# Where the slot-table products stand among the shared expert's projections in a two-layer hybrid trunk step

## Chip, cores and metric

## What is computed

The reference runs two layers over 128 context tokens and 512 latent tokens of width 1024. Each layer has a mixer sub-layer (differential attention, a bidirectional state-space branch and neighbourhood attention) and a channel sub-layer. The change touches only the channel sub-layer:

```python
def moe_ffn(h, p):
    t = h.reshape(-1, d)
    s = jax.nn.sigmoid((t @ p["w_router"]).astype(jnp.float32))
    _, idx = lax.top_k(s + p["b_router"].astype(jnp.float32), TOP_K)
    sel = jnp.take_along_axis(s, idx, axis=-1)
    w = sel / jnp.sum(sel, axis=-1, keepdims=True) * ROUTE_SCALE
    ...
    routed = jnp.einsum("nef,efd->nd", jax.nn.silu(hg) * hu * gates[:, :, None], p["w_e_down"])
    shared = (jax.nn.silu(t @ p["w_s_gate"]) * (t @ p["w_s_up"])) @ p["w_s_down"]
    return (routed + shared).reshape(bn, l, d)
```

There are 32 routed experts with hidden width 128, of which every token takes four, and one shared expert with hidden width 256.

## The kernel before

Each engine has its own instruction stream, written out by hand in program order; the streams meet only at semaphores. Each layer passes a chain of stages. The change is in `stage_tail` (from line 2321), which does the output projection, the norm, the router, the shared expert's two input projections and then all routed experts. `stage_combine` follows it.

**Routing.** VectorE turns router scores into a choice mask, ranks and counts (lines 2840 to 2966). Experts are sorted by token count into 8 groups of 4, one expert for each 32-row lane. Each chosen (token, expert) pair gets a slot. Two one-hot arrays encode it: `where` (the slot tile, L2937 on VectorE and then L2475 on GpSimd, semaphore `where_ready`) and `place` (the position within 128 slots, L2943 on VectorE, semaphore `place_ready`; it lies in the buffer `late`). TensorE multiplies them: 20 products of 128x128 weights by 60 columns summed into PSUM bank 6 (L2611), then `table_mm`. VectorE turns that sum into token numbers and destinations (L2957 to L2966, `table_known`).

**Shared expert.** `shared_lat(c, up)` (L2569, matmuls on L2572) is one projection of the 512 latent tokens: 8 matmuls, one for each k, with 128x128 weights of ring slot 3 and 512 columns, into a PSUM bank of its own (bank 4c + up). Four such calls exist: (0,0), (0,1), (1,0), (1,1). After (0,1) and after (1,1) TensorE raises `shared_mm`; ScalarE answers with Silu (L2741, L2742), and VectorE with the product (L2835, L2836, `shared_hid`).

**TensorE's order around the change** (L2600 to L2617): (0,0), (0,1), two small transposes (L2604), (1,0), then waits for `place_ready` and `where_ready`, the table products, (1,1), `shared_mm`, and `slots_free` raised to 2. Then come `turn(0)` and `turn(1)` (L2619, transposes on L2627), each behind the gather of its 128 rows (`xg_ready0`, `xg_ready1`), and the loop over the expert groups: `up` (L2640), `turn_hidden` (L2647), `turn` of a later tile, `down` (L2658).

**GpSimd** waits for `table_known` and issues two indirect gathers from `h_rows` (L2483), then `gather(2)` and `gather(3)` (L2451), each of which waits until the tile two before it has been transposed. Each gather brings up to 128 rows of 4 KB into `xg` (in the buffer `mixT`). They use DMA queue q0.

**SyncE** loads expert weights over queue q1 (`load_up` L2414, `load_down` L2419; 512 KB each, 12 for each group): group 0 once the experts are known, group 1 once `slots_free` is 2 (it overwrites the shared weights), and each later group once the group two before has passed TensorE. **ScalarE** loads gate rows over queue q10 (L409 to L411) after `turned(1)` and `table_known`.

Of the kernel before, what the change touches and what calls it, by code (L numbers as in the profile page):

```python
# [22 lines left out]
KT = D // P  # L23
# [2297 lines left out]
def stage_tail(nc, cx, L, m, x):  # L2321
# [3 lines left out]
    sem = cx.sem  # L2325
    ps = cx.ps
    with ExitStack() as st:
# [170 lines left out]
        def _(pe):  # L2498
# [67 lines left out]
            pe.sem_inc(sem("slots_free"), 1)  # L2566
            sh = section_ready(cx, pe, ("shared_up", 0)).rearrange("p (k n) -> p k n", k=KT)

            def shared_lat(c, up):  # L2569
                a = up * SFF + c * P  # L2570
                for k in range(KT):
                    ins = pe.matmul(ps[:, 4 * c + up, :], sh[:, k, a:a + P], cx.hT[:, k, CTX:TOK], start=(k == 0),  # L2572
                                    stop=(k == KT - 1))
                return ins

            def shared_ctx(c):
# [21 lines left out]
                sem("rank_mm"), 1)  # L2598
            rows_high(TILES - 1)
            shared_lat(0, 0)  # L2600
            shared_lat(0, 1).then_inc(sem("shared_mm"), 1)
            pe.wait_ge(sem("ids_ready"), 1)
            for j in range(2):
                ins = pe.transpose(ps[0:1, 7, j * P:(j + 1) * P], ids[:, j:j + 1], cx.ident)  # L2604
            ins.then_inc(sem("ids_turned"), 1)
            shared_lat(1, 0)
            pe.wait_ge(sem("rows_high_out"), TILES)
            pe.wait_ge(sem("place_ready"), 1)
            pe.wait_ge(sem("where_ready"), 1)
# [1 line left out]
                ins = pe.matmul(ps[:, 6, 0:TABLE], place[:, n, :], where[:, n, :], start=(n == 0),  # L2611
                                stop=(n == N_CHOICE - 1))
            ins.then_inc(sem("table_mm"), 1)
            shared_lat(1, 1).then_inc(sem("shared_mm"), 1)
            pe.wait_ge(sem("shared_mm"), 2)
            pe.sem_inc(cx.ring_free, 1)
            pe.sem_inc(sem("slots_free"), 1)  # L2617
# [774 lines left out]
```

## Time and profile before

| | before |
|---|---|
| runs | 2551.98, 2555.4, 2559.52 us |
| median | 2555.4 us |
| profiled execution, its own time | 2552.58 us |
| its span in the trace | 2550.8 us |
| TensorE matmul busy | 2374.8 us, 93% |
| VectorE, ScalarE, GpSimd busy | 938.5, 647.4, 412.6 us |
| mean granted TensorE clock | 0.972 of full |

The trace covers the span; the profiled execution's own time is 1.8 us more. Times in timelines count from the start of the span. The channel sub-layer's table products start at 1041.86 us in the first layer and at 2258.22 us in the second. A granted clock of 1.00 is 2.4 GHz, 0.50 is 1.2 GHz.

### The profile page before, as it was taken

How to read it: one execution, taken by the hardware profiler on the slowest of the kernel's cores; microseconds unless marked ns; L12 is line 12 of the kernel's file. 1: busy time of each engine (PE TensorE's matmuls, PEld its weight loads, DVE VectorE, ACT ScalarE, POOL GpSimd, SP SyncE). 2: the span in 40 equal slices, each digit the busy share in tenths (PEclk: the TensorE clock that was granted, in tenths of full speed). 3: DMA queues.
4: the chain of work that ended last, by engine and by line, in shares of the span. 5: the costliest groups of instructions: out<-in, count | busy, mean ns of one | idle time of the engine just before them, and what ended most of it. 6: DMA issues, size and time to landing. Idle time of an engine off the chain costs nothing. (4 is left out here: it accounts for less than half of the span.)

```text
span 2550.8 us, 36359 instructions
## 1 busy us (share of the span) xinstructions
PE 2374.8 (93%) x13824; PEld 1413.1 (55%) x13824; DVE 938.5 (37%) x1813; ACT 647.4 (25%) x1574; POOL 412.6 (16%) x488
## 2 busy tenths in 40 slices
PE   7999999999998999899879999999999899989995
PEld 4446644566457655555455565556655765555552
DVE  2513412552007334422365153246300743452226
ACT  2224401450015013022132252037001501302221
POOL 0003100030003300133410030002100230013333
PEclk8999999999999999899989999999999999989997
DMA  9443145100644220689652220220042322065985
GB/s 348 173 164 102 58 169 214 42 1 33 213 137 110 72 70 34 262 328 401 250 216 88 87 104 33 85 74 1 33 131 76 107 86 70 34 234 207 374 333 221
DMA packets 170190, 368.37 MB, mean 144 GB/s; under 512 B 38836, under 2 KB 52156, under 8 KB 170052
## 3 DMA queue, kind: packets, MB, share of 16 engines
q1 hardware_dynamic: 121604, 261.23, 27.9%
q10 hardware_dynamic: 24768, 54.82, 6.1%
q0 software_dynamic: 23680, 50.43, 5.9%
q8 instruction: 91, 1.49, 0.2%
q14 instruction: 47, 0.39, 0.0%
HBM read 343.99 MB, written 47.56 MB: 154 GB/s over the span
## 5 line engine op out<-in xcount | busy, mean ns | idle before, releaser
L224 PE MATMUL ps<-hT,ring 128*128 128x512 f32 x496 | 222.9, 603 | 5.6 <-PEq L1242 2.7
L233 PE MATMUL ps<-ring,hT 128*128 128x512 f32 x480 | 213.5, 602 | 5.6 <-PEq L1286 4.4
L2640 PE MATMUL ps<-ring,mixT 128*32 128x256 f32 x2688 | 212.5, 379 | 0.6 <-DMA ring<-in_w_e_up 0.4
L2640 PEld LDWEIGHTS ps<-ring,mixT 128*32 128x32 f32 x2688 | 119.4, 110 | 92.9 <-issue 18.1
L224 PEld LDWEIGHTS ps<-hT,ring 128*128 128x128 f32 x496 | 92.8, 192 | 124.0 <-issue 123.9
L233 PEld LDWEIGHTS ps<-ring,hT 128*128 128x128 f32 x480 | 90.8, 192 | 117.8 <-issue 115.9
L1389 PE MATMUL ps<-late,ring 128*128 128x320 f32 x512 | 144.1, 440 | 3.7 <-PEq L1907 2.5
L2508 PE MATMUL ps<-ring,mixT 128*128 128x512 f32 x320 | 140.4, 598 | 4.4 <-PEq L1286 4.4
L1389 PEld LDWEIGHTS ps<-late,ring 128*128 128x128 f32 x512 | 98.1, 193 | 47.6 <-issue 8.2
L756 PE MATMUL ps<-hT,ring 128*128 128x512 f32 x256 | 114.5, 601 | 2.9 <-ACT ssm_dec L1011 2.9
L2658 PE MATMUL ps<-ring,ex_hidT 128*32 128x512 f32 x768 | 115.4, 598 | 0.8 <-DMA ring<-in_w_e_down 0.8
L2010 PE MATMUL ps<-hT,ring 128*128 128x512 f32 x256 | 113.3, 595 | 0.3 <-issue 0.3
L1352 PE MATMUL ps<-mix_T,mix_S 128*128 128x320 f32 x384 | 107.2, 434 | 1.8 <-POOL mix_S L1340 1.2
L2508 PEld LDWEIGHTS ps<-ring,mixT 128*128 128x128 f32 x320 | 60.8, 192 | 79.1 <-issue 79.1
L1949 POOL DMA_DIRECT2D na_raw<-rpb_scratch x64 | 38.1, 598 | 398.9 <-DVE na_bias L2250 291.0
L1352 PEld LDWEIGHTS ps<-mix_T,mix_S 128*128 128x128 f32 x384 | 72.5, 190 | 34.3 <-POOL mix_S L1340 2.2
L1580 POOL TENSOR_SCALAR da_co<-da_sm,da_rc,da_ls 128x1 f32<-128x1 f32 x32 | 11.0, 344 | 480.3 <-DVE da_rc L1864 480.3
L2978 DVE TENSOR_TENSOR ex_hid<-ps,ex_silu 128x128 f32<-128x128 f32 x60 | 17.5, 292 | 188.3 <-ACT ex_silu L2755 188.3
L2640 PE MATMUL ps<-hT,mixT 128*32 128x256 f32 x768 | 85.0, 379 | 0.0
L2640 PE MATMUL ps<-out_xn,mixT 128*32 128x256 f32 x384 | 84.8, 379 | 0.0
L756 PEld LDWEIGHTS ps<-hT,ring 128*128 128x128 f32 x256 | 48.2, 192 | 58.0 <-issue 57.9
L2010 PEld LDWEIGHTS ps<-hT,ring 128*128 128x128 f32 x256 | 47.4, 190 | 58.2 <-issue 58.2
(487 smaller groups left out, 4152.0 us busy)
## 6 DMA issues: line engine op xcount, KB each, us to landing
ring<-in_w_in SPq DMA_DIRECT2D x18, 2048.0 KB, 9.4
ring<-in_w_gate SPq DMA_DIRECT2D x12, 2048.0 KB, 8.7
ring<-in_w_e_down SPq DMA_DIRECT2D x48, 512.0 KB, 14.3
ring<-in_w_e_gate SPq DMA_DIRECT2D x40, 512.0 KB, 7.3
ring<-in_w_e_up SPq DMA_DIRECT2D x40, 512.0 KB, 8.4
mixT<-in_w_ada ACTq DMA_DIRECT2D x8, 2048.0 KB, 8.6
da_ada_w<-in_w_ada ACTq DMA_DIRECT2D x8, 2048.0 KB, 8.6
co_yg<-y_rows SPq DMA_DIRECT2D x28, 512.0 KB, 5.7
```

The lines of the kernel that those rows point to most:

```text
L224: pe.matmul(lat, wide[:, k, c], hT[:, k, CTX:TOK], start=(k == 0), stop=(k == kt_n - 1))
L233: last = pe.matmul(out, cx.hT[:, k, tok(t)], wide[:, k, :], start=(k == 0), stop=(k == KT - 1))
L756: ins = pe.matmul(ps[:, 6, :], wide[:, k, (m % 4) * P:(m % 4 + 1) * P], cx.hT[:, k, CTX:TOK], start=(k == 0), stop=(k == KT - 1))
L1352: ins = pe.matmul(ps[:, bank(q, i), 0:HALF], left[:, k, :], right[:, k, :], start=(k == 0), stop=(k == KH - 1))
L1389: ins = pe.matmul(ps[:, BR + 2 * c + x, 0:HALF], wb[:, k, (2 * q + c) * P:(2 * q + c + 1) * P], cx.oT[:, k, half], start=(k == 0), stop=(k ...
L1580: pool.tensor_scalar(co[:, u % 2:u % 2 + 1], sm[:, u % 3, 0:1], rc[:, u % 3, 1:2], ls[:, 5:6], ALU.mult, ALU.mult).then_inc(sem("da_co"), 1)
L1949: eng.dma_start(raw[:, n % 4, :], src).then_inc(sem(f"na_raw{n % 4}"), 16)
L2010: ins = pe.matmul(ps[:, n % 2, :], wide[:, k, (n // 2) * P:(n // 2 + 1) * P], cx.hT[:, k, CTX:TOK], start=(k == 0), stop=(k == KT - 1))
L2508: ins = pe.matmul(ps[:, 2 * (t % 2) + n, :], cx.mixT[:, k, tok(t)], wide[n][:, k, :], start=(k == 0), stop=(k == KT - 1))
L2640: ins = pe.matmul(ps[rows, 2 + b, 0:2 * P].rearrange("p (g f) -> p g f", g=2), xT[:, b, k, rows], ew[:, :, k, :], start=(k == 0), stop=(k ...
L2658: ins = pe.matmul(ps[rows, 4 + 2 * b + h, :], hidT[:, b, rows], slots[LANES * (s % 2) + c][1][:, h * SEC:(h + 1) * SEC], start=True, stop= ...
L2978: dve.tensor_tensor(hid[:, b, :], ps[:, 2 + b, P:2 * P], silu[:, b, :], ALU.mult).then_inc(sem("tile_hid"), 1)
```

## The change

The call (1,1) of `shared_lat` is cut into two calls of four k each. The first stands ahead of the table products, the second behind them. The accumulation over k in PSUM bank 5 is left open across the table products, which write bank 6. Nothing is added or removed on any engine; only TensorE's order changes.

```diff
-            def shared_lat(c, up):
+            def shared_lat(c, up, ks=range(KT)):
                 a = up * SFF + c * P
-                for k in range(KT):
+                for k in ks:
                     ins = pe.matmul(ps[:, 4 * c + up, :], sh[:, k, a:a + P], cx.hT[:, k, CTX:TOK], start=(k == 0),
                                     stop=(k == KT - 1))
                 return ins
...
             shared_lat(1, 0)
+            shared_lat(1, 1, range(0, KT // 2))
             pe.wait_ge(sem("rows_high_out"), TILES)
             pe.wait_ge(sem("place_ready"), 1)
             pe.wait_ge(sem("where_ready"), 1)
...
             ins.then_inc(sem("table_mm"), 1)
-            shared_lat(1, 1).then_inc(sem("shared_mm"), 1)
+            shared_lat(1, 1, range(KT // 2, KT)).then_inc(sem("shared_mm"), 1)
```

## Rows read from the trace of the kernel before

**Rows 1.** The page: busy time of each engine.

```profile
PE 2374.8 (93%) x13824; PEld 1413.1 (55%) x13824; DVE 938.5 (37%) x1813; ACT 647.4 (25%) x1574; POOL 412.6 (16%) x488
```

**Rows 2.** Timeline, layer 0: start us, us, engine line op out<-in xcount [idle before <-releaser].

```profile
1010.34 3.82 PE L2580 MATMUL ps<-hT,ring 128*128 128x128 f32 x32
...
1030.80 7.03 PE L2572 MATMUL ps<-hT,ring 128*128 128x512 f32 x16
...
1038.93 2.82 DVE L2943 TENSOR_TENSOR late<-route_iota,route_spot 128x2560 f32<-128x2560 f32 x1
...
1041.86 8.76 PE L2611 MATMUL ps<-route_where,late 128*128 128x60 f32 x40 [4.03 <-DVE late L2943]
...
1045.16 0.28 DVE L2836 TENSOR_TENSOR shared_hidden<-ps,route_silu 128x128 f32<-128x128 f32 x1
...
1050.41 9.56 PE L2572 MATMUL ps<-hT,ring 128*128 128x512 f32 x16
...
1052.96 1.09 POOL L2483 DMA_INDIRECT mixT<-h_rows,token_of_slot  x1 [14.09 <-DVE row_of_slot L2966]
...
1060.39 0.33 SPq L2414 DMA_DIRECT2D ring<-in_w_e_gate  x1
...
1060.42 1.06 PE L2627 MATMUL ps<-base,mixT 128*128 128x128 f32 x8 [0.45 <-PE ps L2572]
...
1062.44 1.06 PE L2627 MATMUL ps<-base,mixT 128*128 128x128 f32 x8 [0.95 <-DVE mixT L2972]
1062.60 1.02 POOL L2451 DMA_INDIRECT mixT<-h_rows,ex_index  x1 [0.85 <-POOL ex_index L2446]
...
1063.74 7.11 PE L2640 MATMUL ps<-ring,mixT 128*32 128x256 f32 x128 [0.24 <-issue]
...
1073.01 1.09 PE L2627 MATMUL ps<-base,mixT 128*128 128x128 f32 x8 [1.89 <-DMA mixT<-h_rows,ex_index]
```

**Rows 3.** Timeline, layer 1, the same columns, TensorE alone.

```profile
2258.22 8.76 PE L2611 MATMUL ps<-route_where,late 128*128 128x60 f32 x40 [4.04 <-DVE late L2943]
...
2266.78 8.95 PE L2572 MATMUL ps<-hT,ring 128*128 128x512 f32 x16
...
2276.21 1.06 PE L2627 MATMUL ps<-base,mixT 128*128 128x128 f32 x8 [0.48 <-PE ps L2572]
...
2289.03 1.09 PE L2627 MATMUL ps<-base,mixT 128*128 128x128 f32 x8 [2.34 <-DMA mixT<-h_rows,ex_index]
```

**Rows 4.** Stretches: us, busy of each engine, then PEclk, DMA share, GB/s.

```profile
1037.90:1041.80 3.90, 0.00 (x0) 0.00 (x0) 3.87 (x3) 0.00 (x0) 0.97 (x1) 0.99 0.94 321
1041.80:1046.00 4.20, 4.14 (x20) 4.17 (x20) 3.47 (x8) 0.00 (x0) 0.00 (x0) 0.50 1.03 416
...
1053.00:1056.00 3.00, 3.00 (x6) 1.25 (x5) 0.00 (x0) 0.00 (x0) 2.06 (x2) 0.60 0.36 87
...
2286.70:2289.00 2.30, 0.00 (x0) 0.00 (x0) 0.29 (x1) 0.31 (x2) 0.00 (x0) 1.00 1.00 376
```

**Rows 5.** TensorE's waits, 1042 to 1250: total us, times, longest us.

```profile
PE ps L2627 <- DMA mixT<-h_rows,ex_index: 4.8, 4, 1.9
...
PE ps L2658 <- DMA ring<-in_w_e_down: 0.8, 1, 0.8
```

**Rows 6.** DMA: issue to landing by line: L2483, all L2451, L2451 at 2278.38, L2419.

```profile
DMA to landing us min/median/max: 4.4/4.9/5.4
...
DMA to landing us min/median/max: 2.1/7.6/12.4
...
mixT<-h_rows,ex_index POOLq DMA_INDIRECT x1, 10.6
...
DMA to landing us min/median/max: 9.9/15.3/24.2
```

**Rows 7.** DMA tenths in 40 slices of 1048.6 to 1054.6; then queues of 1062.6 to 1067.

```profile
DMA  9989999999989999998676532200000000000000
...
q1 hardware_dynamic: 461, 1.67, 101.4%
```

## The prediction

> **What bounds the kernel now.** I read the page first: TensorE is busy for 93% of the span [rows 1], so time goes where TensorE's own order leaves a hole or slows. Then the timeline around the moved lines, in both layers. TensorE ends the third shared projection at 1037.83 us (1030.80 + 7.03) and stands idle for 4.03 us until VectorE has written `place`, which ends at 1041.75; the second layer has the same hole, 4.04 us [rows 2, 3]. Third, the stretches with their granted clock. In the hole it is still 0.99; from 1041.8 it is 0.50, that is 1.2 GHz, and the mean of 0.60 over 1053 to 1056 puts its return to 2.4 GHz 0.6 us before the end of that stretch, at 1055.4 [rows 4]. So the hole costs three times: 4.0 us of idleness, 40 table records at 219 ns each (8.76 / 40), and a last projection of 9.56 us (8.95 in layer 1) where the one before took 7.03 [rows 2, 3]. Fourth, what follows the table: TensorE's first row transposes start 0.45 us after the last projection and never waited for their gather, so today TensorE's order, not the gather, sets that start [rows 2].
>
> **The change, part by part** (layer 0; layer 1 repeats it).
>
> *Half a projection into the hole.* 8 of 16 records at 0.43 us (half of 7.03, 3.5 us) run from 1037.8 to 1041.3, before `place` is there at 1041.75. The table still starts at 1041.86, so this costs nothing; the cover is 0.5 us. `table_mm` is awaited by VectorE alone; queued behind TensorE's wait are the same products as before, less the moved half.
>
> *The table at which clock.* TensorE now idles only 0.5 us ahead of it. An idle stretch of 2.30 us further on left the clock at 1.00 [rows 4], so I take full clock. The bounds for 40 records: 8.76 us if the clock is 0.50 regardless, 40 x 119 ns = 4.76 us by the 32 records with equal weights and 128 columns at full clock (3.82 us) [rows 2], and half of 8.76, 4.38, if everything scales with the clock. I take 4.38: weights of that shape are loaded in both, and 60 columns stream less than 128. The table ends at 1046.24 instead of 1050.62.
>
> *From the table to the first gather.* VectorE's conversion and GpSimd's issue follow 2.34 us behind the table's end (1052.96 - 1050.62) [rows 2]; neither depends on TensorE's clock. VectorE's shared product, which stands ahead of it, ends at 1045.44, 0.8 us before the new table end [rows 2]. So the first gather is issued at 1048.6 and the second 1.4 us later, at 1050.0. TensorE finishes the second half of the projection at 1046.2 + 3.5 = 1049.7.
>
> *What is late next: the gather.* TensorE is free 10.3 us earlier than before but can only use what the gather allows. Before, the two gathers went out when the queues were nearly empty and landed after 4.4 and 5.4 us [rows 6]. At 1048.6 the engines are full with group 0's weights for 22 slices of 0.15 us more, to about 1052 [rows 7]. Behind them, group 1's weights come at once: SyncE issued them at 1060.39, right after the last projection [rows 2], and will now issue at about 1050.1. A gather issued into such traffic (1062.60) showed a queue q1 that held all engines for 4.4 us, with not one packet of the gather [rows 7]; its twin of layer 1 landed after 10.6 us, and the slowest after 12.4 [rows 6]. So the landing lies between 4.4 and 10.6 us for the first, 5.4 and 12.4 for the second. I take the middle, 7.5 and 8.9, because the backlog is about to end in the new place and did not end in the old one; the median of all 64 loop gathers is 7.6 [rows 6]. `turn(0)` then starts at 1048.6 + 7.5 = 1056.1 (before: 1060.42, so 4.3 us gained), and TensorE idles 6 us ahead of it.
>
> *The clock falls after all, later.* That hole is longer than the 4.03 us that halved the clock before, so I expect 0.50 through `turn(0)` and most of `turn(1)`. At half clock each takes 1.06 us more; with 0.95 us for the copies between them, `turn(1)` starts at 1056.1 + 3.1 = 1059.2, past the second landing (1058.9). The first `up` follows 1.30 us behind `turn(1)` at full clock, 2.3 at half: 1061.5 instead of 1063.74, 2.2 us gained. The clock came back 5.0 us after dense products began (1055.4 against 1050.4) [rows 2, 4], here at about 1061.1, so `up` runs at full clock.
>
> *Given back to TensorE: the wait for gather 2.* `turn(2)` waited 1.89 us (2.34 in layer 1) [rows 2, 3]. Gather 2 follows `turn(0)` by 2.2 us, 3.2 at half clock, so it is issued at 1059.3, further from the start of group 1's loads, and ahead of ScalarE's gate rows. With 10.6 us it lands at 1069.9, with 7.6 at 1066.9; TensorE gets there at 1061.5 + 9.3 - 1.9 = 1068.9. So `turn(2)` starts between 1068.9 and 1069.9 instead of 1073.01: 3.1 to 4.1 us, middle 3.6. Layer 1 by the same steps: table end 2262.6, gather 2264.9, `turn(0)` 2272.4, `up` 2277.8, `turn(2)` 2285.2 to 2286.3 instead of 2289.03: 2.7 to 3.8, middle 3.3.
>
> *Later groups.* Group 1's weights start 10 us sooner while TensorE is 3 to 4 us sooner, and every later load is released by TensorE's own progress; TensorE waited only 0.8 us for down weights in the loop [rows 5]. I cost this at nothing. If that cover were gone the cost would be of the size of these waits, about 1 us.
>
> **Sum:** 3.6 + 3.3 = 6.9, say 7.0 us, off the profiled execution's 2552.6 us (span 2550.8 plus 1.8): 2545.6. The median is 2.8 us above that execution; I take the same difference from it: 2555.4 - 7.0 = 2548.4 us.
>
> **Rivals.**
>
> *B, the gathers slip in quickly.* Then they land after 4.4 and 5.4 us, at 1053.0 and 1055.4. `turn(0)` starts 7.4 us earlier and `turn(1)` and `up` 7.0, if the clock holds, and up to 2 us less if it falls: 5 to 7 us per layer, 12 in all, 2543.4. For it: the backlog of group 0 ends around 1052 anyway. Against it: the 4.4 us without a packet [rows 7]. The Trainium skill (DMA: Bandwidth & Descriptors, section Queues, rings and completion order) says that each DMA engine serves its queue rows in turn, a packet at a time, which would let a gather in beside a full q1 at once; the trace of before disagrees with that for the first 4.4 us.
>
> *C, no gain.* The gathers land after 10.6 and 12.4 us: 1059.2 and 1062.4, against transposes at 1060.42 and 1062.44. The saved time turns wholly into a wait for the gather. 0 us, 2555, give or take 2.
>
> *D, the change doesn't do what it says:* the table runs at 0.50 although the hole is filled, because the clock falls during its products. The table then ends at 1050.6 as before and only the shorter second half gains: gather at 1052.96 as now, landing 5 us later at 1058.0, 2.4 us per layer, 2550.6. For it: the clock did not recover during 8.8 us of table products. Against it: a clock that stays low is no evidence for one that falls.
>
> *E, slower: the gathers queue behind group 1's weights.* SyncE's 12 loads of 512 KB now go out at 1050.1, within 1.5 us of both gathers, where they used to come after them. Break-even is a first landing 11.8 us after issue (1060.42 - 1048.6). If the gathers take what down weights take, 15.3 us in the median [rows 6], `turn(0)` starts at 1063.9, 3.5 us later than before, and the longer hole brings half clock, another 1 to 2 us: 9 to 10 us in all, 2565. Against it: none of the 64 gathers took over 12.4 us [rows 6].
>
> The Trainium skill (TensorE: Matmul & The Clock Gate, section HAM oscillation) describes a kernel that the DMA wait ahead of each short burst sends back to half clock every time. It speaks against this change, and the forecast already holds one such fall, by the length of the 4.03 us hole.
>
> **How the numbers follow.** The forecast case A has 0.50, B 0.22, C 0.13, D 0.08, E 0.07. About 0.3% (7.7 us, a time below 2547.7) is what a measurement of this kernel can tell from no change, and A's own range, 4 to 10 us (2545 to 2551), straddles it: half of A, 0.25, and all of B make faster 0.47. The rest of A, C and D make same 0.46. E makes slower 0.07. The range reaches over A, most of B and D, and the nearer part of C: 2541 to 2556.
>
> **What would show it.** Right: ahead of the table an idle time of about 0.5 us, table records of about 110 ns apart, 4.4 us in all, at PEclk 1.00; the first gather issued near 1048.6; a new idle time of about 6 us ahead of the first L2627, ended by DMA `mixT`; PEclk 0.50 within it and through the transposes; no or little wait at `turn(2)`. Wrong: a table of 8.8 us (D), no idle time over 3.5 us and landings under 5.5 (B), landings over 10 (C, E), or new waits for expert weights in the loop.

## The result, and the profile after the change

The changed kernel takes 2539.9 us in the median of six runs (2535.1 to 2544.7) against 2554.4 us before (2545.8 to 2559.5). The ratio is 0.9941, with a 95% interval of 0.9921 to 0.9962: faster by 0.6%. The forecast was 2548.4 us with a range of 2541 to 2556, so the direction held and the size did not; the time lies 1.1 us below the range. The profiled execution took 2537.6 us, its span is 2535.8 us.

TensorE's timeline of the first layer in the changed kernel (lines below 2607 have moved down by one, so L2612 is the old L2611, L2628 the old L2627, L2641 the old L2640):

```profile
1026.52 0.38 PE L2604 MATMUL ps<-base,route_ids 128*1 128x128 f32 x2
1026.74 10.47 PE L2572 MATMUL ps<-hT,ring 128*128 128x512 f32 x24
1037.81 4.65 PE L2612 MATMUL ps<-route_where,late 128*128 128x60 f32 x40 [0.60 <-issue]
1042.29 3.65 PE L2572 MATMUL ps<-hT,ring 128*128 128x512 f32 x8
1050.43 1.94 PE L2628 MATMUL ps<-base,mixT 128*128 128x128 f32 x8 [4.49 <-DMA mixT<-h_rows,token_of_slot]
1053.81 1.97 PE L2628 MATMUL ps<-base,mixT 128*128 128x128 f32 x8 [1.43 <-DMA mixT<-h_rows,token_of_slot]
1055.70 7.81 PE L2641 MATMUL ps<-ring,mixT 128*32 128x256 f32 x128
1063.44 0.33 PE L2648 MATMUL ps<-base,ex_hid 128*128 128x128 f32 x1
1063.61 1.04 PE L2628 MATMUL ps<-base,mixT 128*128 128x128 f32 x8
...
1067.05 1.07 PE L2628 MATMUL ps<-base,mixT 128*128 128x128 f32 x8 [0.30 <-DMA mixT<-h_rows,ex_index]
```

Against [rows 2]: the hole of 4.03 us ahead of the table is 0.60, the table takes 4.65 instead of 8.76, the half projection behind it 3.65. Then stands a new hole of 4.49 us, ended by the gather, and both transposes take 1.94 and 1.97 instead of 1.06 each. The wait of 1.89 us at `turn(2)` is gone.

The stretches of the same layer (us, busy of each engine, PEclk, DMA share, GB/s) show the clock that goes with it, as [rows 4] did:

```profile
1037.81:1042.20 4.39, 4.39 (x40) 4.39 (x40) 3.40 (x8) 0.00 (x0) 0.00 (x0) 1.00 1.03 422
...
1045.94:1050.40 4.46, 0.01 (x1) 0.00 (x0) 0.89 (x2) 0.77 (x2) 1.00 (x1) 0.99 1.00 389
1050.40:1053.80 3.40, 1.94 (x8) 1.57 (x8) 0.69 (x1) 0.60 (x1) 0.50 (x2) 0.50 1.02 414
1053.80:1057.10 3.30, 3.29 (x24) 2.27 (x28) 0.69 (x1) 0.60 (x1) 1.11 (x3) 0.50 1.03 412
```

1.00 (2.4 GHz) through the table, 0.50 (1.2 GHz) through the transposes. The half-clock stretch of 13.6 us (1041.8 to 1055.4) has moved behind the table and become about 7 us. In the second layer it begins within the first transposes, which take 1.52 us there.

The gathers, with SyncE's first load for group 1 between them and the landings of the L2483 gathers as far as the trace has them (as [rows 6]):

```profile
1044.79 1.09 POOL L2483 DMA_INDIRECT mixT<-h_rows,token_of_slot  x1 [9.98 <-DVE row_of_slot L2967]
...
1046.19 1.00 POOL L2483 DMA_INDIRECT mixT<-h_rows,token_of_slot  x1 [0.31 <-issue]
1046.36 0.34 SPq L2414 DMA_DIRECT2D ring<-in_w_e_gate  x1
...
DMA to landing us min/median/max: 5.5/7.3/7.6
```

The transposes start 5.6 and 7.6 us behind the issue of their gathers. Before, these landed after 4.4 to 5.4 us. How they came through is in the queues: of 1044.8 to 1047 (first line), of 1047 to 1049 (the next two), and for comparison in the kernel before, from the issue of its first gather at 1052.96 to 1054.7 (last line):

```profile
q1 hardware_dynamic: 243, 0.90, 102.4%
...
q0 software_dynamic: 136, 0.50, 66.7%
q1 hardware_dynamic: 81, 0.26, 33.1%
...
q1 hardware_dynamic: 8, 0.03, 4.1%
```

From its issue at 1044.8 the first gather has no packet for 2.2 us; then its 0.5 MB takes two thirds of the engines for 2 us, beside q1, which still has work. The last line shows that a gather has no packet at first even when the queues are nearly empty: the traces of before have 1.8 us from issue to first packet in both layers. So the full q1 delayed the start here by 0.4 us (by 0.8 in the second layer, where it took 2.6), and of the 4.4 us in [rows 7] only some 2.7 can be put down to it.

**How much of the 15 us is the change?** The two profiled executions differ by 15.0 us, but 4.06 us of that lie ahead of the first small transposes (L2604: 1030.58 before, 1026.52 after), where nothing was changed. So I count each layer from its L2604 to the first product of `stage_combine`. For before:

```profile
1030.58 0.38 PE L2604 MATMUL ps<-base,route_ids 128*1 128x128 f32 x2
1261.29 1.19 PE L3039 MATMUL ps<-shared_down,shared_hidden 128*128 128x512 f32 x1 [9.80 <-PEq L2327]
2246.93 0.38 PE L2604 MATMUL ps<-base,route_ids 128*1 128x128 f32 x2
2500.96 2.04 PE L3039 MATMUL ps<-shared_down,shared_hidden 128*128 128x512 f32 x2 [10.46 <-PEq L2327]
```

That is 230.71 and 254.03 us. After, the same records start at 1026.52, 1251.12, 2238.08 and 2485.96: 224.60 and 247.88 us. So the change gives 6.1 us in each layer, 12.3 in all, and the other 2.8 us of these two executions lie in stretches that it does not touch.

### The profile page after: what moved, and what is told of

Read it like the earlier page. It is cut to its first block and busy times, and to the rows that moved or that the text cites. A ratio compares the mean times of both kernels' runs of the same rounds, so it can differ in the third digit from the quotient of the medians.

```text
span 2535.8 us, 36359 instructions
## 1 busy us (share of the span) xinstructions
PE 2364.8 (93%) x13824; PEld 1403.0 (55%) x13824; DVE 938.2 (37%) x1813; ACT 647.0 (26%) x1574; POOL 411.7 (16%) x488
## 3 DMA queue, kind: packets, MB, share of 16 engines
q1 hardware_dynamic: 121604, 261.23, 28.2%
## 5 line engine op out<-in xcount | busy, mean ns | idle before, releaser
L2641 PE MATMUL ps<-ring,mixT 128*32 128x256 f32 x2688 | 214.1, 382 | 1.4 <-DMA ring<-in_w_e_up 1.4
L2641 PEld LDWEIGHTS ps<-ring,mixT 128*32 128x32 f32 x2688 | 117.6, 111 | 97.2 <-issue 20.7
L224 PEld LDWEIGHTS ps<-hT,ring 128*128 128x128 f32 x496 | 93.3, 193 | 125.0 <-issue 125.0
L2641 PE MATMUL ps<-hT,mixT 128*32 128x256 f32 x768 | 85.0, 379 | 0.0
L2641 PE MATMUL ps<-out_xn,mixT 128*32 128x256 f32 x384 | 84.8, 379 | 0.0
L2628 PE MATMUL ps<-base,mixT 128*128 128x128 f32 x512 | 69.7, 281 | 14.4 <-DMA mixT<-h_rows,token_of_slot 12.0
L2010 PEld LDWEIGHTS ps<-hT,ring 128*128 128x128 f32 x256 | 47.4, 190 | 58.2 <-issue 58.2
```

What stands on the lines that cost most here:

```text
L224: pe.matmul(lat, wide[:, k, c], hT[:, k, CTX:TOK], start=(k == 0), stop=(k == kt_n - 1))
L2010: ins = pe.matmul(ps[:, n % 2, :], wide[:, k, (n // 2) * P:(n // 2 + 1) * P], cx.hT[:, k, CTX:TOK], start=(k == 0), stop=(k == KT - 1))
L2628: ins = pe.transpose(ps[:, k // 4, (k % 4) * P:(k % 4 + 1) * P], xg[:, b, k * P:(k + 1) * P], cx.ident)
L2641: ins = pe.matmul(ps[rows, 2 + b, 0:2 * P].rearrange("p (g f) -> p g f", g=2), xT[:, b, k, rows], ew[:, :, k, :], start=(k == 0), stop=(k ...
```

## Experiments

The stretch from L2604 to `stage_combine` is called the stage below; it is worked out from each trace in the same way.

**The kernel before, again** (no edit).

> The kernel before, once more, for a second trace. From the first table product of a layer to the first product of stage_combine the traces so far show 219.4 us (layer 0) and 242.7 us (layer 1) before, 213.3 and 236.6 after. If this stretch is steady from run to run it is within 0.5 us of 219.4 and 242.7 here; the time ahead of the first layer's table, in which the trace of after was 4.05 us shorter although nothing was changed there, may differ by some us.

Measured: 2555.7 us; stage 230.96 and 255.17 us. The first L2604 is at 1033.84, 3.3 us later than in the first trace. The stage repeats within 0.25 us in layer 0 and 1.1 in layer 1, where I had allowed 0.5; what lies ahead of it varies by several us. So a difference of 1 us between single traces of the stage shows nothing.

**The change, again** (no edit).

> The changed kernel once more. From the two small transposes (L2604) to the first product of stage_combine the traces show 230.7 and 231.0 us (layer 0), 254.0 and 255.2 (layer 1) for the order of before, 224.6 and 247.9 for the change. If the effect lies there and the remaining difference of the first two profiled executions (about 3 of 15 us) was chance, this stretch is again 224 to 225.5 and 247 to 249, and the ratio to before over more runs is 0.995 to 0.996 (12 us) rather than 0.994.

Measured: ratio 0.9955 (0.9939 to 0.9970), median 2542.2 against 2553.9; stage 223.72 and 248.21. The effect is where it was, 7.1 and 6.4 us against the mean of the two traces of before (230.8, 254.6), 13.5 in all. The ratio makes 11.5 us of it, with an interval of 7.7 to 15.6.

**Fill the hole and move nothing.** To the order of before:

```diff
             pe.wait_ge(sem("rows_high_out"), TILES)
+            for k in range(4):
+                pe.matmul(ps[:, 6, :], sh[:, k, 0:P], cx.hT[:, k, CTX:TOK], start=True, stop=True)
             pe.wait_ge(sem("place_ready"), 1)
```

> The order of before, with four extra float32 matmuls (8 records of 512 columns, results overwritten) in the hole ahead of the table products; no work is moved. Theory 1 (the whole gain is the clock that stays at 2.4 GHz through the table; the moved half projection only turns into a wait for the gather): table 4.6 us, last projection 7.0 us, its end 11.5 us behind the table's start, first row transposes 12 us behind it with little or no wait at full clock, stretch from table to combine 5 to 7 us shorter than before in each layer, ratio to before about 0.995. Theory 2 (the gain is the 3.5 us of work moved into the hole, the clock a side matter): nothing is moved, so at most 2 to 3 us in each layer, ratio 0.998 or more.

Measured: ratio 0.9968 (0.9952 to 0.9985), median 2542.5 against 2550.8; stage 224.13 and 249.79, that is 6.7 and 4.8 us shorter than the mean of before, with 3.5 us of work added to each layer.

```profile
1034.57 3.60 PE L2609 MATMUL ps<-hT,ring 128*128 128x512 f32 x8
1038.71 4.68 PE L2613 MATMUL ps<-route_where,late 128*128 128x60 f32 x40 [0.55 <-DVE late L2945]
1043.22 7.09 PE L2572 MATMUL ps<-hT,ring 128*128 128x512 f32 x16
1052.07 1.07 PE L2629 MATMUL ps<-base,mixT 128*128 128x128 f32 x8 [1.76 <-DVE shared_hidden L2838]
...
2275.98 1.49 PE L2629 MATMUL ps<-base,mixT 128*128 128x128 f32 x8 [2.63 <-DMA mixT<-h_rows,ex_index]
```

The table runs at full clock and so does the whole projection behind it, 7.09 us where the order of before took 9.56. The first transposes come 24.6 us behind L2604, in the change 23.9. So in the traces the clock alone makes 5.8 of the 6.6 us per layer (means over both layers, for the change over both of its traces), and the 3.5 us of moved work 0.8, which is no more than the stage varies by. The measured ratio is less sharp: it makes 8.2 us in all, between the two theories (0.995 and 0.998), and its interval holds 0.998 and not 0.995. Theory 2 falls by the trace, not by the ratio: its limit was 2 to 3 us per layer, and the stage is 6.7 and 4.8 us shorter with nothing moved. The first expert products even begin 1.1 to 1.3 us earlier than in the change (28.05 and 27.61 us behind L2604 against 29.18 and 28.90). The clock did fall further on, in layer 0 within the second transposes (their 1.51 us, and 8.29 us for the first expert products), in layer 1 at `turn(2)`, behind an idle time of 2.63 us (the last line above). (The wait of 1.76 us is put down to a VectorE product; the first gather, issued at 1045.72, is the later event, since the trace has 6.0 to 6.2 us for the landings that it records.)

**The whole last projection ahead of the table.**

```diff
-            shared_lat(1, 1, range(0, KT // 2))
+            shared_lat(1, 1).then_inc(sem("shared_mm"), 1)
...
-            shared_lat(1, 1, range(KT // 2, KT)).then_inc(sem("shared_mm"), 1)
```

> The whole last projection (8 matmuls) ahead of the table products, nothing behind them. The products reach 3.0 us past place_ready, so table, gather issue and first transposes each come 3.0 us later than in the changed kernel, and TensorE idles about 8 us for the gather. Theory 1 (the chain table, gather, transposes sets the time): stretch from table to combine, counted from the end of VectorE's place, 3 us longer than after, still 2 to 4 us shorter than before, ratio to before 0.997. Theory 2 (TensorE's work is the bound): the same as after, 0.994.

Measured: ratio 0.9994 (0.9978 to 1.0010); stage 231.95 and 253.51, the same as before.

```profile
1025.36 0.38 PE L2604 MATMUL ps<-base,route_ids 128*1 128x128 f32 x2
1025.58 13.90 PE L2572 MATMUL ps<-hT,ring 128*128 128x512 f32 x32
1039.32 4.57 PE L2612 MATMUL ps<-route_where,late 128*128 128x60 f32 x40
1054.28 1.94 PE L2627 MATMUL ps<-base,mixT 128*128 128x128 f32 x8 [10.39 <-DMA mixT<-h_rows,token_of_slot]
1057.17 1.94 PE L2627 MATMUL ps<-base,mixT 128*128 128x128 f32 x8 [0.95 <-DVE mixT L2972]
1059.04 9.21 PE L2640 MATMUL ps<-ring,mixT 128*32 128x256 f32 x128
...
DMA to landing us min/median/max: 7.9/9.0/9.1
...
q1 hardware_dynamic: 481, 1.75, 102.5%
```

The table starts 13.96 us behind L2604 instead of 11.29, 2.7 us later, as reckoned. But the transposes come 5.0 us later than in the change (28.9 against 23.9), because the last projection now ends before the table, so that SyncE's first load for group 1 goes out at 1042.11, 4.1 us ahead of the first gather (1046.23); the gathers land after 7.9 to 9.1 us. The first of them has no packet from 1046.23 to 1050.5, while q1 holds the engines (the last line above), so the 4.4 us of [rows 7] come back here. This is the traffic of rival E, at a smaller price. The hole of 10.39 us brings half clock, and the first expert products take 9.21 us. The direction (the chain counts, not TensorE's sum of work) held. The cost was too small: 6.6 us per layer against the change instead of 3. Of the difference, 2.3 us are the later landings, which I had not reckoned with, and 1.4 the first expert products at half clock (9.21 against 7.81 us).

**Two of eight k ahead of the table.**

```diff
-            shared_lat(1, 1, range(0, KT // 2))
+            shared_lat(1, 1, range(0, 2))
...
-            shared_lat(1, 1, range(KT // 2, KT)).then_inc(sem("shared_mm"), 1)
+            shared_lat(1, 1, range(2, KT)).then_inc(sem("shared_mm"), 1)
```

> The last projection cut after 2 of 8 k instead of 4: 1.7 us of work in the hole, 5.2 us behind the table. Idle about 2.3 us ahead of the table and 2.8 us ahead of the first transposes, instead of 0.6 and 4.5. Theory 1: the clock stays at 1.00 through both, since idle stretches of 2.3 us kept it in the trace of before; the second transposes and the first expert products run at full clock, 1.5 us per layer less than after. Rival (any idle time of 2 us or more ahead of sparse products brings 0.50): the table takes up to 8.8 us, 3 to 5 us per layer more than after.

Measured: ratio 0.9978 (0.9961 to 0.9996); stage 228.07 and 252.36, 4 us per layer more than the change.

```profile
1037.97:1040.28 2.31, 0.00 (x0) 0.03 (x1) 2.31 (x2) 0.00 (x0) 0.00 (x0) 1.00 1.02 401
1040.28:1046.60 6.32, 6.32 (x41) 6.32 (x41) 3.41 (x8) 0.00 (x0) 0.00 (x0) 0.70 1.02 416
1046.60:1053.40 6.80, 6.80 (x13) 2.78 (x13) 1.33 (x7) 0.00 (x0) 2.10 (x2) 0.78 0.80 289
...
1057.22 7.11 PE L2641 MATMUL ps<-ring,mixT 128*32 128x256 f32 x128 [0.24 <-issue]
...
1067.46 1.97 PE L2628 MATMUL ps<-base,mixT 128*128 128x128 f32 x8 [2.87 <-DMA mixT<-h_rows,ex_index]
1069.36 3.64 PE L2659 MATMUL ps<-ring,ex_hidT 128*32 128x512 f32 x16
```

The clock outlives the hole of 2.31 us and falls within the table behind it (0.70 as a mean), so the table takes 6.5 us. My expectation was wrong there, and the rival had the price right, 3 to 5 us per layer. But the slow table is not where the time goes. The gathers are issued 1.9 us later (20.13 us behind L2604 against 18.27), when group 0's loads are done, and land after 4.3 to 5.4 us, so the first expert products begin 28.2 us behind L2604, 1 us earlier than in the change, and at full clock. The loss comes after them: TensorE waits 2.87 us for gather 2 (3.40 in layer 1) where the change did not wait, and the clock falls again: 1.97 us for the transposes instead of 1.04, 3.64 for the first down products instead of 1.92. `turn(2)` comes 1.4 us later than in the change and `turn(3)` 3.7 (44.20 against 40.53). Gather 2 is issued where it was in the change (27.07 us behind L2604 against 26.96), but group 1's loads began 2.2 us ahead of it here and 7.1 us there; that this is why it landed later is argued, not shown.

What idle time the clock bears is not settled by this. 1.89 to 2.59 us ahead of `turn(2)` left it at 1.00 in all four layers of the two traces of before; 2.63 us at the same place, with nothing added there, was followed by a fall in the run with the filled hole, and 2.87 and 3.40 here.

**Group 1's weights released later.** To the changed kernel:

```diff
             pe.wait_ge(sem("shared_mm"), 2)
             pe.sem_inc(cx.ring_free, 1)
-            pe.sem_inc(sem("slots_free"), 1)
...
             turn(0)
             turn(1)
+            pe.sem_inc(sem("slots_free"), 1)
```

> The changed kernel, but slots_free, on which SyncE loads group 1's expert weights, is raised behind the second row transposes instead of ahead of the first: the two gathers no longer share the engines with group 1's weights. If that traffic is what makes them land after 5.5 and 7.5 us, they land after about 4.5 and 5.5 here, the first transposes start 1 us and the second 2 us sooner. Gather 2 then meets the weights from their start and lands later (10 us against under 10), so the stretch from L2604 to stage_combine is within 1.5 us of the change. If the traffic of group 0 alone delays them, the landings stay at 5.5 and 7.5.

Measured: ratio 0.9945 (0.9927 to 0.9963); stage 223.24 and 247.82; landings:

```profile
DMA to landing us min/median/max: 4.5/5.3/5.3
```

So group 1's weights cost the second gather some 2.2 us (5.3 against 7.3 to 7.8 in the two traces of the change), and the first nothing that shows: in layer 0 its transposes start 5.65 us behind its issue here and 5.64 in the change. The 4.5 is the first gather of layer 1, which went out behind a slow table, when group 0's loads were done. I had expected 1 us on the first and 2 on the second. The second transposes start 26.0 us behind L2604 in layer 0 instead of 27.3, but the first expert products then run at half clock for longer (8.95 us), and the stage gains 0.4 to 0.5 us over the change run again, less than the 0.9 by which the two traces of the change differ. In layer 1 of this execution the clock fell within the table in spite of a full hole:

```profile
2254.97 6.32 PE L2612 MATMUL ps<-route_where,late 128*128 128x60 f32 x40 [0.60 <-issue]
2261.09 5.34 PE L2572 MATMUL ps<-hT,ring 128*128 128x512 f32 x8
```

The stage of this layer is no longer for it than that of the change (247.82 against 247.88 and 248.21 us): the table ends 1.7 us later, but the gathers land after 4.5 and 5.3 us, and the first expert products take 7.11 us at full clock instead of 8.0 to 8.3.

**Keep TensorE busy while it waits for the gather.** To the changed kernel:

```diff
+            pe.wait_ge(sem("experts_known"), 1)
+            filler = where[:, :, :].rearrange("p n s -> p (n s)")[:, 0:SEC]
+            for _ in range(4):
+                pe.matmul(ps[:, 7, :], cx.ones, filler, start=True, stop=True)
             pe.wait_ge(sem("shared_hid"), 1)
             turn(0)
```

> The changed kernel with four extra float32 matmuls of constants (8 records, 3.4 us, into a bank that nobody reads then) between the last projection and the first row transposes, where TensorE idles 4.5 us for the gather. They cost nothing if they end before the gather lands, and keep the idle time to about 1 us. If the fall to 0.50 there costs what the rows say (second transposes 1.97 against 1.06 us, first expert products 7.8 to 8.0 against 7.1), the stretch from L2604 to stage_combine is 1.5 us per layer shorter than the change, 3 us in all, ratio 0.994. If the wait for later gathers or weights takes it back, it is the same as the change.

Measured: ratio 0.9956 (0.9939 to 0.9973), no different from the change; stage 227.96 and 249.42, longer than that of the change run again by 4.2 and 1.2 us.

```profile
1048.11 1.06 PE L2628 MATMUL ps<-base,mixT 128*128 128x128 f32 x8 [0.41 <-DMA mixT<-h_rows,token_of_slot]
1052.49 1.76 PE L2628 MATMUL ps<-base,mixT 128*128 128x128 f32 x8 [3.32 <-DMA mixT<-h_rows,token_of_slot]
1054.18 8.07 PE L2641 MATMUL ps<-ring,mixT 128*32 128x256 f32 x128
...
PE ps L2641 <- DMA ring<-in_w_e_up: 3.3, 1, 3.3
```

The first transposes ran at full clock, and then the second gather, landing 8.5 us after issue, made a hole of 3.32 us and the clock fell there. The last line, TensorE's longest wait for weights between 1040 and 1245 us, shows where more time went in layer 0: 3.3 us for up weights of a later group. In layer 1 the clock stayed at full through both transposes and the first expert products (7.11 us), and the stage was no shorter for it. By the ratio the extra products cost nothing and buy nothing while the gathers share the engines.

**Both.** The two edits above together.

> Both: the extra matmuls of e4_keep_warm and the later slots_free of e3_late_slots. If gathers and clock each cost what was argued, the second transposes start 2 us sooner and run at full clock, the first expert products start 3 us sooner than in the change; the wait for gather 2 or for group 1's weights, which now start 8 us later, gives back 1 to 3 us of it. Forecast 0 to 2 us per layer shorter than the change; longer, if group 1's weights are late (a new wait on L2641 for in_w_e_gate or in_w_e_up would show it).

Measured: ratio 0.9940 (0.9923 to 0.9956), median 2539.7; stage 222.80 and 247.63.

```profile
1054.72 1.06 PE L2627 MATMUL ps<-base,mixT 128*128 128x128 f32 x8 [0.61 <-DMA mixT<-h_rows,token_of_slot]
1056.73 1.06 PE L2627 MATMUL ps<-base,mixT 128*128 128x128 f32 x8 [0.95 <-DVE mixT L2977]
1058.21 7.11 PE L2640 MATMUL ps<-ring,mixT 128*32 128x256 f32 x128 [0.42 <-issue]
```

Every step of the start-up is at full clock: the first expert products begin 27.4 us behind L2604 and take 7.11 us (change run again: 29.4 and 7.67). Of these 2.6 us the waits for gathers 2 and 3 and for weights take most back, and the stage is 0.6 to 0.9 us shorter, which is no more than the change's own two traces differ by. Against the change the ratio overlaps, so it is not shown to be faster.

## Why the prediction was wrong in size

The chain of reasoning held step by step up to the landings. The step that failed is what the first gathers pay for beside the weights' loads: their landing was taken as 7.5 and 8.9 us and measured 5.3 to 5.6 and 7.3 to 7.8, so the gain was sized too small. Two smaller terms, the wait at `turn(2)` and what lies behind it, were too small as well.

- *Half a projection into the hole, at no cost.* Right: the table starts 11.29 us behind L2604 after and 11.28 before.
- *The table at full clock, 4.38 us.* Right to 0.3 us: all 40 records begin within 4.37 us at 1.00, and by the count that gave 8.76 before the table takes 4.65. The clock, on the table and on the projection behind it, makes most of the gain, as the filled hole without moved work shows (5.8 us per layer). The Trainium skill's account (TensorE: Matmul & The Clock Gate, section HAM oscillation) of bursts set back by the wait ahead of them fits the order of before (a wait of 4.03 us) as much as the new hole (4.49 us).
- *From the table to the first gather, 2.34 us; second half done behind it.* Right: 1044.79 is 2.33 us behind the table's end at 1042.46. TensorE finishes at 1045.94, 8.1 us behind the table's start, as reckoned (1049.7 against 1041.86: 7.8).
- *What is late next: the gather.* Right as a mechanism, a new hole ended by DMA `mixT`. **This term was mis-sized:** I took 7.5 and 8.9 us from the middle between quiet and contended gathers; the transposes started 5.6 and 7.6 us behind the issues in layer 0, 5.3 and 7.4 in layer 1. The first transposes gained 5.9 us in layer 0 (29.85 to 23.91 behind L2604) instead of 4.3. My reason, that a gather waits for the backlog of q1, was wrong here: it had packets 2.2 us after issue, beside a q1 that was still full. I had charged the whole 4.4 us of [rows 7] to q1, of which a gather takes 1.8 with the queues nearly empty; here q1 added 0.4 to 0.8. The Trainium skill (DMA: Bandwidth & Descriptors, section Queues, rings and completion order) says that each engine serves its queues in turn. The trace agrees at this place, where q0 had 66.7% and q1 33.1%; the 2.7 us that are left of [rows 7], and 2.5 in the run with the whole projection ahead, are not explained by it. Rival B had it half right: quick for the first gather, not for the second.
- *The clock falls after all, later.* Right for layer 0: 0.99 within the hole, 0.50 through both transposes; in layer 1 it fell within the first. That the first `up` would be at full clock was wrong: the stretch to 1057.1, 6.7 us after the transposes began, is still at 0.50, the next at 0.99, so these products take 7.81 us (8.03 in layer 1) instead of 7.11.
- *Given back at turn(2).* **The second mis-sized term, mostly by way of the first.** I let gather 2 land 7.6 to 10.6 us after issue and end TensorE's wait at 1068.9 to 1069.9, for a gain of 3.6 us. It was issued at 1053.48, TensorE came at 1063.6 and did not wait, so it had landed within 10.1 us: the gain was 5.4 us in layer 0 and 5.1 in layer 1 (42.10 to 37.03). A smaller wait at `turn(3)` (0.30 instead of 0.80 in layer 0, none in layer 1) brings it to 5.9 and 6.1, and that stays to the end of the stage: 6.1 and 6.1. Against the forecast of 3.6 and 3.3 that is 2.5 and 2.8 us more: 1.2 because TensorE reached `turn(2)` earlier than forecast (37.1 us behind L2604 against 38.3), which follows from the first gather's earlier landing; 0.5 because it did not wait there; and 0.8 and 1.1 from `turn(3)` on, which the forecast put at nothing.
- *Later groups at nothing.* The traces show nothing against it. In layer 0 TensorE waited for up weights 0.4 and 1.9 us in the two traces of before, 1.4 and 0.9 in those of the change, and 0.8 to 3.3 in the variants, which is too near to the spread of before to say more.
- *The rivals.* C did not come about. D did not in the change, but it did in one layer of a variant with the hole filled, where the stage was no longer for it. E's traffic is real (2 us on the second gather, more where the loads go out first) but far from its break-even.

Sum: 12.3 us instead of 6.9. The remaining difference to the measured 14.5 us is not attributed; the second comparison, over more runs, gave 0.9955, which is 11.5 us, and both intervals hold 12.3.

What stays open: why a gather had its first packet 2.2 to 2.7 us after issue beside the rest of group 0's loads, and only after 4.2 to 4.9 where group 1's loads had gone out 2 us or more before it (as far as the packets of single gathers can be told apart); and what makes the clock fall within the table in one of the fourteen traced layers that came to it with a hole of 0.6 us or none.

## What to carry to other kernels

A hole in TensorE's order ahead of sparse products can cost more through the clock than through the idle time: here, in layer 0, 4.0 us of idleness and 6.6 us of half clock behind it (4.1 on the table, 2.5 on the last projection), and four throw-away matmuls in the hole recovered most of what moving real work did (11.5 of 13.2 us by the traced stages, 8.2 us against 11.5 and 15.1 by the measured ratios, whose intervals overlap). Before work is moved ahead of a product, follow that product's result to the next transfer and see what is released with it: the whole projection ahead of the table gave the entire gain back. Of the 5.0 us by which its first transposes came later than in the change, 2.7 are the later table; the other 2.3 I put down to the weights' loads, which then went out ahead of the gathers, but no run has that order with the loads held back. A hole that is filled in one place can also open in another: with two of eight k in the hole the time went at `turn(2)`, long behind the table. A gain of this size is best read on the stretch that the change touches, since stretches that it does not touch varied by several us between executions.

## What the runs showed of the hardware

- The same idle time, 2.3 us, left the granted clock at 1.00 ahead of `turn(2)` in the kernel before and was followed by a fall to 0.50 within the table products in another run (6.3 us at 0.70 as a mean). At `turn(2)` itself a fall came with 2.63 us.
- Table products with 128x128 weights and 60 columns start 112 ns apart at 2.4 GHz (4.37 us from the first to the last of 40) and 214 ns apart at 1.2 GHz (8.34 us): 1.9 times as long.
- At 1.2 GHz these products ran for 8.76 us without a pause and the clock did not come back; it came back 5.0 us into the projection behind them in layer 0, 3.7 in layer 1.
- Indirect gathers of 128 rows landed after 4.3 to 5.4 us with nearly empty queues, 5.4 to 8.5 beside weights whose load had just begun, and 7.9 to 9.1 in the middle of such a load. The first packet came 1.8 us after issue in the first case and 4.3 us after it in the last.
- Gather packets, once they came, took 66.7% of the engines against 33.1% of the weights' queue for 2 us.
